# Quarter-row gathers and VectorE transposes in the expert blocks of a hybrid trunk kernel

## What is computed

```python
def _moe(x, router_w, router_bias, w_gate, w_up, w_down, sh_gate, sh_up, sh_down):
    t = x.reshape(bsz * l, d)                                   # 640 x 1024
    scores = jax.nn.sigmoid((t @ router_w).astype(jnp.float32)) # 64 experts
    _, idx = lax.top_k(scores + router_bias.astype(jnp.float32), TOP_K)   # 8 of 64
    sel = jnp.take_along_axis(scores, idx, axis=-1)
    wts = sel / jnp.sum(sel, axis=-1, keepdims=True) * ROUTED_SCALE
    gates = jnp.einsum('tk,tke->te', wts, jax.nn.one_hot(idx, N_EXPERTS, dtype=jnp.float32))
    hid = jax.nn.silu(jnp.einsum('td,edf->tef', t, w_gate)) * jnp.einsum('td,edf->tef', t, w_up)
    routed = jnp.einsum('tef,efd->td', hid * gates[..., None], w_down)
    shared = (jax.nn.silu(t @ sh_gate) * (t @ sh_up)) @ sh_down
    return (routed + shared).reshape(bsz, l, d)
```

## Time and profile before

| | us |
|---|---|
| median of three runs (1451.89 to 1452.76) | 1452.35 |
| span of the profiled execution | 1449.8 |
| TensorE busy | 1337.0 (92%) |
| VectorE busy | 685.5 (47%) |
| ScalarE busy | 412.0 (28%) |
| GpSimd busy | 301.5 (21%) |
| first gate/up of block 0 | at 922.9 |
| last gate/up, block 69 | at 1362.7 |
| first gather of y | at 1374.4 |

### The profile page before, as it was taken

How to read it: one execution, slowest core, us unless ns; L and a number is a source line. 1 busy time by engine, 2 the same in 40 slices (tenths; PEclk the granted TensorE clock), 3 DMA queues, 4 the chain that set the end, 5 groups by cost and what they waited for, 6 DMA issues and landing times. The chain is left out here.

```text
span 1449.8 us, 21596 instructions
## 1 busy us (share of the span) xinstructions
PE 1337.0 (92%) x8160; PEld 996.5 (69%) x8160; DVE 685.5 (47%) x1254; ACT 412.0 (28%) x796; POOL 301.5 (21%) x440
## 2 busy tenths in 40 slices
PE   5999999999899998999799999999999999999664
PEld 1678666777899986555545457688888888887521
DVE  2698738202665663777576226432222222222156
ACT  3212221215556554233131025321222122212111
POOL 0200100102321311454440210211111111111173
PEclk9999999999999999999899999999999999999998
DMA  9656667121433341000120401799999999998696
GB/s 360 209 174 186 201 43 59 58 73 30 182 153 100 127 175 34 8 5 31 37 103 23 175 0 44 281 385 393 384 378 384 378 397 382 398 385 307 212 382 264
DMA packets 111005, 286.36 MB, mean 198 GB/s; under 512 B 28677, under 2 KB 46639, under 8 KB 109528
## 3 DMA queue, kind: packets, MB, share of 16 engines
q1 hardware_dynamic: 95096, 242.15, 48.6%
q0 software_dynamic: 15840, 43.28, 7.8%
HBM read 237.52 MB, written 64.56 MB: 208 GB/s over the span
## 5 line engine op out<-in xcount | busy, mean ns | idle before, releaser
L2771 PEld LDWEIGHTS PS<-arena 128*128 128x128 f32 x2240 | 258.5, 192 | 43.3 <-ACT arena L3310 26.2
L2771 PE MATMUL PS<-arena 128*128 128x128 f32 x2240 | 263.1, 276 | 5.2 <-DMA arena<-in_exp_w_down 3.9
L3098 DVE TENSOR_SCALAR arena<-PS,arena 128x1024 f32<-128x1024 f32 x70 | 89.9, 1284 | 141.6 <-PE PS L2779 141.6
L2779 PE MATMUL PS<-arena 128*128 128x512 f32 x280 | 137.8, 615 | 0.8 <-DVE arena L3091 0.8
L895 PE MATMUL PS<-arena 128*128 128x320 f32 x384 | 109.4, 438 | 1.5 <-DVE arena L1317 1.5
L3316 ACT ACTIVATE arena<-PS 128x128 f32<-128x128 f32 x70 | 19.4, 277 | 312.7 <-issue 176.7
L900 PE MATMUL PS<-arena 128*128 128x320 f32 x384 | 107.3, 432 | 0.0
L3091 DVE TENSOR_TENSOR arena<-arena,PS 128x128 f32<-128x128 f32 x70 | 20.1, 288 | 182.8 <-ACT arena L3316 93.4
L895 PEld LDWEIGHTS PS<-arena 128*128 128x128 f32 x384 | 73.0, 192 | 33.3 <-issue 2.9
L900 PEld LDWEIGHTS PS<-arena 128*128 128x128 f32 x384 | 73.0, 190 | 30.4
L3403 POOL DMA_INDIRECT arena<-h_rows,arena x70 | 72.1, 1030 | 58.4 <-POOL arena L3400 57.6
(11 more groups left out here) (478 smaller groups left out, 2078.0 us busy)
## 6 DMA issues: line engine op xcount, KB each, us to landing
arena<-in_exp_w_gate SPq DMA_DIRECT2D x70, 512.0 KB
arena<-in_exp_w_up SPq DMA_DIRECT2D x70, 512.0 KB
arena<-in_exp_w_down SPq DMA_DIRECT2D x70, 512.0 KB
y_rows<-arena SPq DMA_DIRECT2D x70, 512.0 KB
arena<-in_w_in SPq DMA_DIRECT2D x16, 1024.0 KB, 6.2
arena<-in_w_mod SPq DMA_DIRECT2D x32, 512.0 KB, 3.7
y_rows<-cst SPq DMA_DIRECT2D x2, 5632.0 KB, 18.5
y_rows<-cst SPq DMA_DIRECT2D x2, 5120.0 KB, 18.0
```

The lines of the kernel that those rows point to most:

```text
L2771: mm = pe.matmul(PS[:, bank, 0:P], w[:, k, :], xT[j % 2][:, k, :], start=k == 0, stop=k == KT - 1)
L2779: mm = pe.matmul(PS[:, 4 + 2 * (j % 2) + half, :], hid[j % 2], ed[j][:, 512 * half:512 * half + 512], start=True, stop=True)
L3098: dve.tensor_scalar(yb[j].rearrange("p (h n) -> p h n", h=2), PS[:, 4 + 2 * (j % 2):6 + 2 * (j % 2), :], gate_col[j % 2], None, ALU.mult). ...
```

## The change

- The HBM copy of the rows has no gates, and each row is stored as four quarters: quarter a holds, for each of the eight parts k of x, 32 words. `h2_rows` is 2560 rows of 256 words. ScalarE writes `h2` in that order.
- The table holds four row numbers per block and partition: partition 32a+s, number g, is quarter a of the token in slot 32g+s. Building it takes four 128x128x106 products with spread identities and two VectorE steps.
- A block's x is fetched by four indirect DMAs of 128 quarter rows (1 KB each). VectorE turns them with one instruction of 32x32 transposes (turn_x), issued two blocks ahead. TensorE's transposes and ScalarE's copy of them go.
- gate_up alternates between two pairs of PSUM banks, with two `gact`. TensorE's order is gate_up(b), down(b-1), in the regular and in the spill blocks.
- y is evicted unscaled by ScalarE. The 40 gates are picked out by VectorE (gates_of, in blocks 5 to 9) and applied in the final sum: ScalarE scales choice 0 and makes 20 scaled identities for TensorE's choices 4 to 7, VectorE multiplies and adds choices 1 to 3.
- The 64 regular blocks are unrolled on every engine; the spill blocks stay loops. SP's loads and stores keep their order and their waits.

```diff
-ROW_W = D + NE
+QROW = D // 4
...
-        xg = [part(r1_at + ROW_W * i, ROW_W) for i in range(U)]
+        xg = [part(r1_at + D * i, D).rearrange("p (g c) -> p g c", g=4) for i in range(U)]
...
-                with sp.Fori(1, NE // U) as i:
-                    for j in range(U):
-                        sp.wait_ge(e_ps, U * i + (j + 1 - U))
-                        load_block(U * i + j, j)
-                        store_block(U * i + (j - U), j)
+                for b in range(U, NE):
+                    sp.wait_ge(e_ps, b - U + 1)
+                    load_block(b, b % U)
+                    store_block(b - U, b % U)
...
+                pe.wait_ge(m_slots, 2)
+                for g in range(4):
+                    mm = pe.matmul(PS[:, 7, COLS * g:COLS * g + COLS], spread_ident[g].rearrange("p a s -> p (a s)"), slots, start=True, stop=True)
+                mm.then_inc(m_rows, 1)
...
-                with pe.Fori(1, NE // U) as i:
-                    for j in range(U):
-                        transpose_x(j, i + 1)
-                        down(U * i + (j - 1), (j - 1) % U)
-                        gate_up(U * i + j, j, i + 1)
+                for b in range(NE):
+                    gate_up(b, b % U, b // U + 1)
+                    if b:
+                        down(b - 1, (b - 1) % U, b <= 2)
 
                 def spill(i, before):
-                    transpose_x(0, i + (NE // U + 1))
+                    gate_up(2 * i + NE, 0, i + (NE // U + 1))
                     down(2 * i + (NE - 1), before)
-                    gate_up(2 * i + NE, 0, i + (NE // U + 1))
-                    transpose_x(1, i + (NE // U + 1))
+                    gate_up(2 * i + (NE + 1), 1, i + (NE // U + 1))
                     down(2 * i + NE, 0)
-                    gate_up(2 * i + (NE + 1), 1, i + (NE // U + 1))
...
+                def turn_x(b, j, fetched):
+
+                    dve.wait_ge(e_x[j], 64 * fetched)
+                    if b is not None:
+                        dve.wait_ge(e_gu, b - 1)
+                    dve.transpose(xT[j % 2].rearrange("p k (g s) -> p g k s", s=32),
+                                  xg[j].rearrange("p g (k i) -> p g k i", i=32)).then_inc(e_xT, 1)
...
+                for b in range(NE):
+                    hidden(b, b % U, b < 2)
+                    if b + 2 < NE:
+                        turn_x(b + 2, (b + 2) % U, (b + 2) // U + 1)
...
+                def take_y(b, j, free=None):
+                    act.wait_ge(e_ps, b + 1)
+                    if free is not None:
+                        act.wait_ge(e_out[j], free)
+                    act.activation(yb[j].rearrange("p (h n) -> p h n", h=2), PS[:, 4 + 2 * (j % 2):6 + 2 * (j % 2), :],
+                                   ACT.Copy).then_inc(e_y, 1)
...
+                def gather(j, rows):
+
+                    for g in range(4):
+                        pool.indirect_dma_start(xg[j][:, g, :], None, T["h2_rows"], bass.IndirectOffsetOnAxis(rows[:, g:g + 1], 0),
+                                                bounds_check=4 * TOK - 1, oob_is_err=False).then_inc(e_x[j], 16)
+
+                for b in range(NE):
+                    if b >= U:
+                        pool.wait_ge(e_xT, b - U + 1)
+                    gather(b % U, quarter_row[:, b, :])
...
-                    dve.tensor_tensor(acc[:, t, :], first, second, ALU.add).then_inc(g_dve, 2)
...
+                        dve.scalar_tensor_tensor(out=acc[:, t, :], in0=row, scalar=gate_of[:, t, k:k + 1], in1=acc[:, t, :],
+                                                 op0=ALU.mult, op1=ALU.add).then_inc(g_dve, 1)
```

228 lines of the change are left out of this document (116 added, 112 removed).

## The result

| | us |
|---|---|
| kernel before, median of 4 runs beside it (1451.89 to 1453.06) | 1452.55 |
| changed kernel, median of 4 runs (1509.38 to 1517.13) | 1512.07 |
| ratio, 95% interval | 1.0417 [1.0398, 1.0437] |
| span of the profiled execution, before and after | 1449.8 and 1507.2 |

The change makes the kernel 4.2% slower, 59.5 us. The forecast was 1469, +1.2%, with 1494 as the upper end: the sign was right, the time lies outside the range.

What follows compares the result with a forecast made beforehand. It took TensorE and the DMA queues to be full at once: blocks -13.4, start 0, spill +23.0, its end +0.6, clock +6.8, tail +0.3, sum +17.3 us; forecast 1469 us, range 1445 to 1494.

Steps and rivals of the forecast that it cites:

- Direction: Whole kernel: slower, chance 0.75; same 0.10, faster 0.15.
- the gain in the blocks: 64 regular blocks: DMA-bound, period from 6.305 to 6.08 us, 14.4 us saved less 1 for descriptors, entered as -13.4.
- Spill: Blocks 66 to 69: new order exposes the load latency of 7.55 us, +23.0 us, plus +6.8 for TensorE's lowered clock.
- The start: Before and during the first blocks: first gate/up 3.6 us later, won back over some six blocks; net zero, -3 to +5.
- 5.3 us against 6.08, hidden: Regular blocks: GpSimd's four indirect DMA issues take 5.3 us, fit within a 6.08 us block and cost nothing.
- rival 3: Regular blocks: GpSimd becomes the bound through longer issues or costly small packets, 6.6 us a block, 1502 us; chance 0.13.
- The rate of the transfers: Regular blocks: DMA engines deliver 396 GB/s, halfway between 388 and 404, giving 6.08 us a block.
- The number of packets: Gathers in regular blocks: four times the packets, costing 0 to 0.12 us a block, 1 us taken in all.
- The clock in the regular blocks: TensorE busy 89% of a regular block; since 88% ran at clock 1.00, no loss there.
- The lead of the loads: Regular blocks: lead falls from three periods to two, about 12 us against 7.5 latency, so it stays hidden.
- Engines that get work: Regular blocks: VectorE's new transpose takes 1.2 us; VectorE, ScalarE and GpSimd work all hidden, costing nothing.
- the end: After the spill blocks: +0.6 us on leaving the spill and +0.3 in the final sum, +0.9 in all.

Runs made afterwards that it cites:

- pacing: Changed kernel with block b's gathers also held until gate/up four blocks before has ended; 1484.5 us, 1.0239 on chip 5, 1486.7 us, 1.0254 on chip 11.
- one_gather: Changed kernel with one indirect DMA of whole 4 KB rows per block instead of four of quarter rows (output not the reference's); 1496.9 us, 1.0336.
- after_again: Changed kernel run once more, unaltered, on chip 11; 1522.0 us, 1.0488.
- paced_old_spill: Changed kernel, gathers held until gate/up four blocks before ended, TensorE's old order in spill blocks; 1432.8 us (0.9883) on chip 3, 1456.2 us (1.0038) on chip 11.
- after_full: Changed kernel with an in-range row number for every slot no token fills, so no empty descriptors; 1496.2 us, 1.0317.
- roll_pe: Changed kernel with TensorE's blocks 4 to 63 back in a loop, other engines unrolled; 1512.9 us, 1.0434.
- roll_all: Changed kernel with SyncE, ScalarE, VectorE and TensorE looping again, only GpSimd unrolled; 1520.4 us, 1.047.
- before_3empty: Kernel before plus three indirect DMAs that move nothing behind each block's gather, the transposes waiting for all four; 1478.2 us, 1.0196.

## Why the prediction was wrong, point by point

**Direction.** The loss was expected in the spill, and the gain in the blocks too small to pay for it. The first is shown; in the blocks there was no gain but a second loss. The step that failed is the price of the four issues: it was counted as GpSimd's own time, 5.3 us "hidden, with 0.8 us to spare", and at nothing for everyone else.

**Spill: right, mechanism and size.** 23.0 + 6.8 = 29.8 us forecast, 30.2 measured, and 30 to 32 us come back with the old order on two chips, with pacing or without. The latency was 7.81 instead of 7.55, the clock took 1.4 to 2.9 us a block instead of 1.7.

**The start: failed.** "Net zero, bounds -3 and +5" was +15.8. The sum there counted four issues of GpSimd as four times their own time. What it left out is that 28 issues in a row, which the four free buffers and the early transposes allow, hold TensorE, ScalarE and SP as well, and that TensorE's clock falls with the stops: 0.64 from 923 to 960 us. With one gather a block gu(4) is 0.1 us from that of before; on chips 3 and 4 it is at 948.6 to 952.3 with runs of 72 to 88, paced or not. On chip 11, pacing alone moved it from 970.2 to 950.7.

**GpSimd: "5.3 us against 6.08, hidden": right for GpSimd, wrong for the rest.** Its issue took 1.00 us, the gap 0.30, four of them 4.9 us; it was busy 209.8 of 340 us, so rival 3 in its own form, GpSimd without idle time, did not happen. Nor did its reason: beside VectorE's transposes the issues had a mean of 1.01 us, against 1.03 before. On the Trainium skill's rule of the port that GpSimd and VectorE share (SBUF — State Buffer, on the shared port pair), no run here shows a lockout for the transpose. That rival's time, 1502, was near by luck: the issues held not GpSimd but its neighbours. What that is worth in a block is known only in part. Pacing gave back 0.41 us of 6.66 on chip 11; but one_gather, in which nothing is held, still took 6.50 on chip 5, with 47.4 us of waits for weights in the place of the stops.

**The rate of the transfers, 396 GB/s between 388 and 404: mis-sized, and its opposite on some chips.** On chip 3, with four gathers a block and nothing held, the engines delivered 405 and 408 GB/s over 340 us and the block took 6.00 and 5.91 us, below the 6.08 forecast and inside its bounds. The 385 to 388 of the earlier trace rows was TensorE's demand, not what the engines could do; it should not have been averaged with the 404. The early 404 was the one row in which the loads had free buffers ahead of TensorE. On chips with pauses kernels with four gathers got 357 to 370 unpaced and 389 to 390 paced; SP, which issues the loads, was among those held up. The kernels with one gather of 4 KB rows had no more than 372 on chip 5 and, with the longer lead, 391 on chip 3, without a hold-up; what keeps them below 405 is open. The figure of 358 GB/s that the Trainium skill gives (DMA: Bandwidth & Descriptors, Specifications) was passed by 14% here for 340 us; the fabric's 435 was not reached.

**The number of packets, "four times": wrong, with little effect.** The records show 193 packets a block against 144. The gathers' queue took 44.4 us a MB in the changed kernel against 40.9 before (share x 16 engines x 340 us over its MB). For the 0.32 MB of a block and 16 engines that is 0.07 us, an estimate, and inside the prediction's bounds of 0 and 0.12.

**The clock in the regular blocks, "so nothing there": failed in part.** It was at 0.50 for 20.5 of the 340 us from 960 on, for 43.5 in after_again, and for 3.4 in the paced kernels. TensorE was busy for 88% of this window, as in the stretch at 1.00 that the prediction leaned on the earlier trace rows, but here its work was broken by stops.

**The lead of the loads, "so it stays hidden": failed, though small where nothing pauses.** Back from two periods to three, the block goes from 6.00 to 5.91 us on chip 3, about 5 us in all. With one gather a block it went from 6.50 on chip 5 to 6.18 on chip 3, 18 us; there chip and edit changed together, so the split between them is open.

**Engines that get work: right.** The transpose, which no row showed, took 1.24 us where 1.2 was taken:

```profile
L3096 DVE STREAM_TRANSPOSE arena<-arena 128x1024 f32<-128x1024 f32 x70 | 86.4, 1237 | 22.8 <-DMA arena<-h_rows,arena 21.8
```

**The whole.** Forecast +17.3, measured +57.4: of the 40.1 between them the start holds 15.8, the blocks 23.5, the end 1.3, and the spill gives 0.5 back. The changed kernel itself never ran on a chip without pauses. From two neighbours it would be near 1464 us there: paced_old_spill with 31 us more for the spill order; or after_full with 0.52 us less per block, its additional bytes. Both are estimates. They lie inside the range, whose upper end was too low for one thing, a cost of the issues to other engines.

**What stays open.** By what GpSimd's issues hold the other engines on chips 5, 9 and 11, and why not on 3 and 4. Unrolling, the supply of instructions and too few bytes in flight are excluded (roll_pe, roll_all; the groups stop where nothing is waited for). before_3empty shows that issues without data can make a silu late, but only two between 960 and 1300 us by more than 2 us, and stops no group; its gathers have gaps of 1 us between blocks. Whether issues without empty descriptors do it was tried only on a chip without pauses. One candidate is in the Trainium skill (NOTIFIC — the notification-queue block, Overflow: three behaviours, one of which stalls the engine): a queue that takes an engine's event records can, when it is full, stall the engine that writes them. Engines that stop in the midst of a group and go on together would look like this; no run here shows it or excludes it, and no run without such records is at hand, so their part in the time is not known.

## What to carry to other kernels

When two steps of a loop change places, look up what each of them releases: a load that was issued ahead of a product is now issued behind it, and in the part of the kernel with the fewest buffers the whole latency comes out, here 7.8 us a block and 30 us in all; releasing each load by its own last reader (two thirds by gate/up, a third by down) covers it in either order. Read the rate of the transfers from a stretch in which they set the pace; where a compute engine does, the rate is its demand. Count four small indirect DMAs in place of a large one as a price for every engine, not only for the one that issues them; holding them back was worth 28 to 35 us on chips with pauses. With paced gathers, early release and the old spill order the idea of the change does pay, 0.9842 [0.9814, 0.9869] and 0.9825 [0.9801, 0.985] on two chips without pauses; on one with pauses only the version without the early release ran, at 1.0038 [1.0015, 1.0061].

## What the runs showed of the hardware

- On three chips, and on that of the first pair, with back-to-back indirect DMAs of GpSimd (1.00 us each, 0.30 between), ScalarE and SP start late (silus by up to 8 us) and mostly go on within 2.3 us of the end of a run. In the changed kernel, with runs of four to fifteen, TensorE stops within groups of products too (32 stops, 19.7 us of 340); in the paced one, with runs of eight, hardly (1.4 us). A run of 28 goes with a first gu(4) that is 15.8 us late. On two other chips runs of 72 to 88 pass without a late silu or a stop. The kernel before, with one gather a block, takes about 1450 us on all of them.
- The records of the two kinds differ elsewhere too. On chips 3 and 4 the profile gives the landing time of the experts' loads, on the others, that of the first two profiles included, it finds none. A row of paced_old_spill:

```profile
arena<-in_exp_w_gate SPq DMA_DIRECT2D x56, 512.0 KB, 7.2
```

- and the same of the changed kernel, without the last column:

```profile
arena<-in_exp_w_gate SPq DMA_DIRECT2D x52, 512.0 KB
```

- The mixture of 1 KB gathered rows, 512 KB loads and stores ran at 405 to 408 GB/s for 340 us on chips 3 and 4, no slower than the whole rows. The rows stand in the records as packets of 4096 B, so this says nothing of packets of 1 KB.
- After 7.8 to 8.1 us without work TensorE's clock stood at 0.50, its lower level of 1.2 GHz, and the next 32 passes took 5.24 and 6.26 us instead of 3.83:

```profile
1384.00:1388.00 4.00, 1.14 (x5) 1.15 (x6) 0.00 (x0) 0.00 (x0) 0.00 (x0) 0.50 0.73 261
```
